# A third seven-product pair in each feed-forward layer, at steps 3, 6 and 8 in place of 5 and 8

## The reference

```python
def swiglu(x, w_in, w_out):
    gate, up = jnp.split(x @ w_in, 2, axis=-1)
    return (jax.nn.silu(gate) * up) @ w_out

for i in range(DEPTH):
    h = layer_norm(DN_ALPHA * h + 0.5 * swiglu(h, ffn_w_in[i, 0], ffn_w_out[i, 0]), ln_g[i, 0], ln_b[i, 0])
    ...
    h = layer_norm(DN_ALPHA * h + 0.5 * swiglu(h, ffn_w_in[i, 1], ffn_w_out[i, 1]), ln_g[i, 2], ln_b[i, 2])
```

## Time and profile before

| | us |
|---|---|
| median of 3 runs (1499.13 to 1499.2) | 1499.16 |
| the profiled execution's own time | 1499.28 |
| its span, first to last instruction | 1497.5 |
| PE busy in the span | 1487.8 (99%) |
| DVE busy | 1074.1 (72%) |
| ACT busy | 814.6 (54%) |
| mean granted TensorE clock | 0.999 |

### The profile page before, as it was taken

The page is one execution under the profiler, slowest core; times in us unless marked ns, Lnnn a source line. Parts: engine busy times, 40 slices in busy tenths (PEclk is TensorE's granted clock), DMA queues, the critical chain, the costliest instruction groups (busy, mean ns, idle before and its releaser), DMA issues.

```text
span 1497.5 us, 18806 instructions
## 1 busy us (share of the span) xinstructions
PE 1487.8 (99%) x7798; PEld 1268.6 (85%) x7798; DVE 1074.1 (72%) x1115; ACT 814.6 (54%) x827; POOL 143.3 (10%) x144
## 2 busy tenths in 40 slices
PE   9999999999999999999999999999999999999998
PEld 8888888888888888888888888888998888888886
DVE  7698677777868688677566768866786466775555
ACT  6465566556556565553434556555645666354443
POOL 0020010200002000024031200002002200020000
PEclk9999999999999999999999999999999999999999
DMA  9773654576657656555544675655444434465551
GB/s 393 255 260 106 246 208 169 204 263 218 218 193 289 228 188 194 207 219 195 177 165 169 257 261 186 195 205 220 169 152 176 152 141 147 162 228 193 197 195 58
DMA packets 45444, 301.71 MB, mean 201 GB/s; under 512 B 5440, under 2 KB 5888, under 8 KB 10672
## 3 DMA queue, kind: packets, MB, share of 16 engines
q1 hardware_dynamic: 38592, 270.35, 48.2%
q0 software_dynamic: 4960, 26.41, 7.5%
q10 hardware_dynamic: 1808, 3.74, 0.7%
HBM read 282.60 MB, written 1.05 MB: 189 GB/s over the span
## 4 chain that ended last, share of the span: by engine, by line
PE 98%; DMA 1%; SPq 0%; issue 0%; ACT 0%; DVE 0%; POOLq 0%; POOL 0%; DVEq 0%
PE psum L2000 16%; PE psum L2003 16%; PE psum L2004 16%; PE psum L2109 13%; PE psum L2113 7%; PE psum L2136 6%; PE psum L2246 3%; PE psum L2247 3%; PE psum L2250 3%; PE psum L2143 3%; PE psum L2032 2%; PE psum L2045 2%; PE psum L2038 2%; PE psum L2012 1%; DMA weights_raw_more<-in_weights 1%; PE psum L2267 0%
## 5 line engine op out<-in xcount | busy, mean ns | idle before, releaser
L1180 DVE TENSOR_TENSOR weights_lo<-weights_raw,weights_hi 128x2048 fp32r<-128x2048 f32 x187 | 431.6, 2312 | 219.6 <-ACT weights_hi L609 218.1
L609 ACT ACTIVATE weights_hi<-weights_raw 128x2048 fp32r<-128x2048 f32 x194 | 364.3, 1882 | 222.7 <-PE psum L2004 136.2
L2000 PE MATMUL psum<-weights_hi,hidden_hi 128*128 128x512 f32 x416 | 163.3, 393 | 0.0
L2003 PE MATMUL psum<-weights_lo,hidden_hi 128*128 128x512 f32 x416 | 162.5, 391 | 0.0
L2004 PE MATMUL psum<-weights_hi,hidden_lo 128*128 128x512 f32 x416 | 162.0, 389 | 0.0
L2000 PE MATMUL psum<-weights_hi,operand 128*128 128x512 f32 x384 | 151.5, 394 | 0.0
L2003 PE MATMUL psum<-weights_lo,operand 128*128 128x512 f32 x384 | 149.9, 390 | 0.0
L2109 PE MATMUL psum<-operand,weights_hi 128*128 128x512 f32 x608 | 144.6, 390 | 0.0
L2004 PE MATMUL psum<-weights_hi,operand 128*128 128x512 f32 x352 | 137.2, 390 | 0.0
L2109 PEld LDWEIGHTS psum<-operand,weights_hi 128*128 128x128 f32 x608 | 112.9, 188 | 22.7
L1180 DVE TENSOR_TENSOR weights_lo<-weights_raw_more,weights_hi 128x2048 fp32r<-128x2048 f32 x52 | 117.8, 2286 | 4.0 <-ACT weights_hi L609 4.0
(11 more groups left out here) (379 smaller groups left out, 2690.5 us busy)
## 6 DMA issues: line engine op xcount, KB each, us to landing
weights_raw<-in_weights SPq DMA_DIRECT2D x194, 1024.0 KB, 4.8
weights_raw_more<-in_weights SPq DMA_DIRECT2D x60, 1024.0 KB, 8.0
weights_raw<-weights_raw_more POOLq DMA_DIRECT2D x8, 1024.0 KB, 11.0
weights_raw<-weights_raw POOLq DMA_DIRECT2D x8, 1024.0 KB, 6.9
ln_rows<-in_ln_rows POOLq DMA_DIRECT2D x16, 512.0 KB, 7.6
weights_raw<-in_weights SPq DMA_DIRECT2D x4, 256.0 KB, 4.0
weights_raw<-in_weights SPq DMA_DIRECT2D x2, 512.0 KB, 5.9
normalised<-in_x POOLq DMA_DIRECT2D x2, 512.0 KB, 12.9
```

Source lines behind the costliest of these rows:

```text
L609: nc.scalar.activation(hi[:, rest], whole[:, rest], ACT.Copy).then_inc(hi_split, 1)
L1180: nc.vector.tensor_tensor(lo_of(n), raw_of(n), hi_of(n).bitcast(F32), ALU.subtract).then_inc(lo_split, 1)
L2000: mm(out, a_hi, b_hi, start=start, stop=False, skip_group_check=True)
L2003: mm(out, a_hi, b_lo, start=False, stop=False, skip_group_check=True)
```

## The change

The pairs of a layer move from steps 5 and 8 to steps 3, 6 and 8. A layer's units after steps 0 and 1 were 2, 3, 4, pair 5/6, 7, pair 8/9, 10; they are now 2, pair 3/4, 5, pair 6/7, pair 8/9, 10. Tables for loads, buffers and operand places follow from `GROUPS`. Two orders written by hand change as well: VectorE splits T1 behind step 2's sums where a pair follows step 2, and in layer 0 ScalarE takes step 0's silu one tile earlier.

```diff
-GROUPS = (5, 8)
+GROUPS = (3,6,8,)
...
                 split_hi(n0 + 3)
                 if f:
                     keep_x((None, 2, 3, 5)[f])
-                split_hi(n0 + 4)
+                if f:
+                    split_hi(n0 + 4)
                 silu(n0, pairs[0][:, :, 0:TOK])
+                if not f:
+                    split_hi(n0 + 4)
                 second_of_next(2, n0 + 5)
...
                     if after in GROUPS:
+                        if j == 2:
+                            split_lo(n0 + GROUP_AT[after] + 1)
                         add_t2(after)
...
                         split_lo(ahead - 1)
                         split_lo(ahead)
-                        if after in GROUPS:
+                        if after in GROUPS and j > 2:
                             split_lo(ahead + 1)
                         summed_step(j, after)
```

## The result

The changed kernel takes **1505.27 us** (median of 15 runs, 1500.33 to 1508.23) against 1499.16 (15 runs, 1498.98 to 1499.93): ratio 1.0038, 95% interval 1.0028 to 1.0047. It is slower by 0.4%. The forecast was 1495.5 with a range of 1491.0 to 1499.5; the time lies above it. The new spread of 8 us, where the kernel before has 1, is itself part of the result. The profiled execution of the changed kernel took 1503.4 us (span 1501.4), near the middle of that spread.

What follows compares the result with a forecast made beforehand. TensorE's work plus its waits bound the kernel. Layer 0 loses 3.2 us, layers 1 to 3 gain 2.32 each, adjacent pairs cost 0: -3.8 us from 1499.28 gives 1495.5, range 1491.0 to 1499.5.

Steps and rivals of the forecast that it cites:

- the landing of T1 of 8/9: Adjacent pairs 6/7 and 8/9: T1 lands 24.5 us after 6/7's start, between 22.2 and 28.0, so TensorE does not wait.
- The limit of 26.3 us: Pair 8/9: latest landing of T1, counted from 6/7's start, that has its down tile ready when due at 47.1 us.
- rival (b): Adjacent pairs wait for T1: each us past 26.3 idles TensorE a us per layer, 1504.0 at worst; chance 0.16.
- Layer 0's first pair: Pair 3/4 in layer 0: T1 lands at 43.4, the pair ends at 82.2 instead of 78.99, losing 3.2 us.
- Layers 1 to 3, T1 of 3/4: T1 has 1.8 us of slack in layer 1, others alike or easier: no cost, each layer keeps 2.32 us.
- The silu edit at nothing: Layer 0: taking step 0's silu earlier removes a 1.3 us wait, counted as nothing: TensorE then waits longer for T1.
- the residual beside T3 and b22: Layer 0's pair 3/4: with POOL's residual alongside, T3 and b22's split take 3.1 us each; without it, chain 1.7 shorter.
- The gain of 2.32 us: Each layer: two plain steps (33.14 us) become one pair (30.82), 2.32 us less TensorE work, 9.28 in four layers.

## Why the prediction was wrong

**The failed step** is the landing of T1 of 8/9: "Fewer loads run beside it than before ..., so I take 24.5, the middle: no wait". Measured were 29.1, 23.5, 30.4 and 25.5 in the order of the layers, with 26.3 as the limit and 28.0 as the prediction's upper bound (13.9 + 14.1). The issue was put too early for every layer and the landing too short for layers 0 and 2. T1 was issued at 15.8, 14.4, 16.0 and 15.2 in place of 13.9: b22's split was taken at 9.0 and came at 9.1 to 10.7 (the row of layer 0 had said 10.6), and the 0.5 us from b12's landing to the issue had hardly a term. From issue to landing T1 then took 13.3, 9.1, 14.4 and 10.3, where 24.5 left it 10.6. A middle was the wrong kind of answer, and it was also misread: the middle of 22.2 and 28.0 is 25.1, and with the split at 10.6 it is 26.7 in layer 0, past the limit.

What decided instead is the load issued next to T1. The eight sums of the earlier trace rows already lay in two groups. In three of the four long ones a load was issued within 0.1 us of T1, in the fourth 1.1 us ahead of it. In the four short ones, which the prediction took for lone sums, the next load came 2.0 to 2.5 us behind; they took 8.3 to 8.4 us, where the run with b22's load held shows 6.9 to 7.5. The long ones had earlier loads still in flight as well, so those eight alone do not separate the two causes. The run that moves b22's load and nothing else does, for layers 0 and 2. The prediction even had the time of that issue: the down tile's split at 16 us frees a buffer. It wrote this down as a sign of little traffic, and it is the moment at which a T1 that is 2 us late is issued.

**The limit of 26.3 us** was right to 0.3 us, and so was rival (b) in its kind: each us past the limit is a us lost, and the sign turns at about a us a layer. Its worst case, 1504.0 with all four layers late, still lies below the median of 1505.27: in the profiled run two late layers alone cost 7.5 of the 8.5 us that it had given to four. Its chance of 0.16 was too low, since it took the long landing in one or two layers for the exception. A smaller term put at nothing is the end of the kernel, 0.65 us longer.

**Layer 0's first pair** was right in its sum, with small errors that partly cancel. T1 was issued at 30.1 (29.7 forecast) and took 12.7 us (13.7, a choice within 8.3 to 16.8): it landed at 42.8 (43.4 forecast), the copies started at 44.69 (45.2), TensorE idled 4.3 us (4.7), VectorE's chain from the copies to the down product took 22.6 (22.5), and the pair ended at 81.87 (82.2). Of the 2 us of idle foreseen inside the pair only 0.24 stood at the down product. The rest was filled by TensorE running slower. The windows show it, and the one other place within the layers where it happened (granted clock: third column from the end; 1 is 2.4 GHz):

```profile
45.00:50.00 5.00, 3.95 (x10) 3.14 (x11) 4.70 (x4) 3.19 (x4) 0.00 (x0) 0.66 0.60 247
...
599.00:603.00 4.00, 4.00 (x12) 3.13 (x11) 4.00 (x3) 2.08 (x2) 0.71 (x1) 0.57 0.79 164
```

Behind the idle time the second block of step 2's down product took 4.45 us (46.05 to 50.50) where it took 2.72 in the earlier trace rows. Since VectorE's chain set the end, this cost nothing there.

**Layers 1 to 3, T1 of 3/4**: right, 2.3 us gained in each and no wait. **The silu edit at nothing** and **the residual beside T3 and b22**: right, each shown by its own run. **The gain of 2.32 us** per pair: right.

## What to carry to other kernels

When a DMA stands on the path, don't take a mean of its landings. Ask which transfer will be issued within a us or so of it, on its own queue too, and look for two groups in the landings that the trace has. If a late transfer would cost more than the gain, give it its inputs earlier, or hold back the load that meets it: either was worth 9 us here. Work off the critical path that frees buffers sets these moments, so two pairs side by side call for a look at each queue as well as at each engine.

## What the runs showed of the hardware that was not expected

**A transfer of 1 MB landing in half the time.** T1 of 8/9, an addition from buffer to buffer, landed in 14.4 and 13.3 us with a load issued 0.2 us ahead of it or at the same moment, in 10.3 and 9.1 with the load 0.7 and 1.4 us behind, and in 6.9 to 7.5 with it 4 to 5.4 us behind. By the Trainium skill (DMA: Bandwidth & Descriptors, section Queues, rings and completion order) each DMA engine takes turns by packet between the queues with work. The trace agrees loosely: T1's 7.5 us and a lone load's 4.8 make 12.3, near the 13.3 of T1 when both started together; but that load took 7.2, and two more loads were issued 4.0 and 4.4 us behind T1. The prediction had held the rule to be contradicted by the earlier trace rows: a T1 that shares need not land near its time alone, so 14.1 us beside loads do not speak against it. Why 1.4 us are enough to spare T1 4 to 5 us is not shown by these runs. Nor is the nearest load the whole rule: T1 of 3/4 in layer 2 of the changed kernel took 10.0 us with a load 1.4 us ahead of it and the next 2.2 us behind, and behind another adding DMA on its own queue T1 took 12.6 to 13.7 us with no load near.

**The clock.** The granted clock fell from 2.4 to 1.2 GHz for a while behind the idle of 4.3 us in layer 0 (0.66 in the mean of 45 to 50 us), behind 2.1 us in layer 2 (0.57 from 599 to 603), and behind 3.1 us in the run with ScalarE's new order (0.66). It did not fall behind the late down tile of the pairs at 4, 6 and 8 (2.7 us of wait, 1.00 from 85 to 90). One length of idle does not tell these apart.

**The tail.** From the start of the last product to the end of the span it is 7.7 us in the three kernels with two pairs a layer, and 8.34 us in all eleven with three. GpSimd's drain at the end takes 3.7 us in the three and 4.36 us in the eleven. The eleven have eight adding DMAs more on its queue. That they are the cause is likely and was not tried.
